# Feed-forward gate and up: wide and narrow products of a weight block in another order

## The reference

```python
def swiglu(h, w_gate, w_up, w_down):
    return (jax.nn.silu(h @ w_gate) * (h @ w_up)) @ w_down

x = x + 0.5 * swiglu(rmsnorm(x, ffn1_norm[i]), ffn1_w_gate[i], ffn1_w_up[i], ffn1_w_down[i])
```

## Time and profile before

| | before |
|---|---|
| median of the three runs | 1577.62 us |
| lowest and highest run | 1577.44, 1578.19 us |
| span of the profiled execution, first to last instruction | 1575.9 us |
| time of the profiled execution itself | not listed apart; the runs lie 1.5 to 2.3 us above its span |
| TensorE busy with products | 1412.2 us, 90% of the span |
| weight loads | 1117.4 us, 71% |
| VectorE, ScalarE, GpSimd | 891.4, 613.8, 33.0 us |
| mean granted TensorE clock | 0.967 of full speed |

### The profile page before, as it was taken

How to read it: one execution, slowest core, us unless ns; L and a number is a source line. 1 busy time by engine, 2 the same in 40 slices (tenths; PEclk the granted TensorE clock), 3 DMA queues, 4 the chain that set the end, 5 groups by cost and what they waited for, 6 DMA issues and landing times.

```text
span 1575.9 us, 25855 instructions
## 1 busy us (share of the span) xinstructions
PE 1412.2 (90%) x10318; PEld 1117.4 (71%) x10318; DVE 891.4 (57%) x1227; ACT 613.8 (39%) x817; POOL 33.0 (2%) x69
## 2 busy tenths in 40 slices
PE   8999999999999999999999999999886666666666
PEld 7888888888888888877788888778653434333333
DVE  5777688577776777765457776777621121121121
ACT  6443465563445543466654344664211001000000
POOL 4000000000000000000010000010000000000000
PEclk9999999999999999999999999999999889989889
DMA  7565543456565555554456556557999999999996
GB/s 239 198 209 191 188 160 134 134 169 218 172 209 164 188 196 197 167 177 142 134 150 214 196 166 211 161 171 271 396 400 427 428 428 428 430 428 429 428 428 291
DMA packets 149044, 396.67 MB, mean 252 GB/s; under 512 B 8003, under 2 KB 106387, under 8 KB 136704
## 3 DMA queue, kind: packets, MB, share of 16 engines
q1 hardware_dynamic: 147424, 392.20, 66.9%
q0 software_dynamic: 1440, 3.72, 1.0%
q10 hardware_dynamic: 128, 0.03, 0.0%
HBM read 393.83 MB, written 1.05 MB: 251 GB/s over the span
## 4 chain that ended last, share of the span: by engine, by line
PE 75%; DMA 19%; DVE 4%; ACT 2%; issue 1%; SPq 0%; ACTq 0%; DVEq 0%; POOL 0%; POOLq 0%
DMA pair_ring<-in_w_exp_up 19%; PE psum L557 17%; PE psum L258 12%; PE psum L260 12%; PE psum L259 12%; PE psum L563 9%; PE psum L2342 6%; PE psum L1024 1%; DVE low L253 1%; PE psum L2369 1%; PE psum L1435 1%; DVE hT L445 1%; ACT hT L435 0%; PE psum L2380 0%; PE psum L424 0%
## 5 line engine op out<-in xcount | busy, mean ns | idle before, releaser
L253 DVE TENSOR_TENSOR low<-raw,high 128x2048 fp32r<-128x2048 f32 x179 | 409.6, 2291 | 193.6 <-ACT high L249 193.1
L249 ACT ACTIVATE high<-raw 128x2048 fp32r<-128x2048 f32 x179 | 341.2, 1910 | 125.1 <-PE psum L563 90.2
L557 PE MATMUL psum<-hT,high 128*128 128x512 f32 x1152 | 288.0, 392 | 0.1
L557 PEld LDWEIGHTS psum<-hT,high 128*128 128x128 f32 x1152 | 209.3, 189 | 39.3 <-DVE low L253 0.4
L2342 PE MATMUL psum<-pair_ring,gain 128*32 128x256 f32 x1984 | 140.2, 445 | 96.1 <-DMA pair_ring<-in_w_exp_up 96.1
L258 PE MATMUL psum<-high,hT 128*128 128x512 f32 x496 | 200.1, 403 | 6.9 <-DVE low L253 4.5
L260 PE MATMUL psum<-high,hT 128*128 128x512 f32 x496 | 194.5, 392 | 0.0
L259 PE MATMUL psum<-low,hT 128*128 128x512 f32 x496 | 193.9, 391 | 0.0
L2342 PEld LDWEIGHTS psum<-pair_ring,gain 128*32 128x32 f32 x1984 | 77.4, 128 | 158.4 <-issue 134.6
L563 PEld LDWEIGHTS psum<-hT,low 128*128 128x128 f32 x1152 | 157.1, 190 | 11.2
L563 PE MATMUL psum<-hT,low 128*128 128x256 f32 x1152 | 160.6, 282 | 0.0
(11 more groups left out here) (356 smaller groups left out, 1452.5 us busy)
## 6 DMA issues: line engine op xcount, KB each, us to landing
pair_ring<-in_w_exp_gate SPq DMA_DIRECT2D x31, 2048.0 KB, 18.9
pair_ring<-in_w_exp_up SPq DMA_DIRECT2D x31, 2048.0 KB, 23.3
pair_ring<-in_w_exp_down SPq DMA_DIRECT2D x31, 2048.0 KB, 24.4
raw<-in_ffn_w_gate SPq DMA_DIRECT2D x88, 512.0 KB, 4.0
raw<-in_ffn_w_up SPq DMA_DIRECT2D x88, 512.0 KB, 5.0
raw<-in_ffn_w_down SPq DMA_DIRECT2D x88, 512.0 KB, 4.3
raw<-in_gla_w_in SPq DMA_DIRECT2D x24, 512.0 KB, 4.5
raw<-in_sb_w_in SPq DMA_DIRECT2D x24, 512.0 KB, 4.7
```

Source lines behind the costliest of these rows:

```text
L249: act.activation(high[:, p % RING, :], raw_of(p), ACT.Copy).then_inc(rounded, 1)
L253: dve.tensor_tensor(low[:, p % RING, :], raw_of(p), high[:, p % RING, :].bitcast(F32), ALU.subtract).then_inc(split, 1)
L557: pe.matmul(to.rearrange("p (o n) -> p o n", o=2), w_high, both_parts, start=kk == 0, stop=False, skip_group_check=True)
```

## The change

The second loop over `k` is taken away. Its body is put into the first one: behind the wide product of (k, i) the narrow product of the same (k, i) is issued. The products, operands, banks, flags and semaphore steps are the same, and the last instruction of a call is still the narrow product of k = 3, i = 1.

```diff
                 kk = 4 * half + k
                 both_parts = hT[:, :, kk * TOKENS:(kk + 1) * TOKENS]
                 for i in range(2):
-                    w_high, _, to = block(k, i)
+                    w_high, w_low, to = block(k, i)
                     pe.matmul(to.rearrange("p (o n) -> p o n", o=2), w_high, both_parts, start=kk == 0, stop=False,
                               skip_group_check=True)
-            for k in range(4):
-                kk = 4 * half + k
-                for i in range(2):
-                    _, w_low, to = block(k, i)
                     ins = pe.matmul(to[:, 0:TOKENS], w_low, hT_high[:, kk, :], start=False, stop=kk == KD - 1,
                                     skip_group_check=True)
             return ins
```

## The result

The changed kernel is slower. Over six runs its median is 1584.48 us, against 1577.53 us for the kernel before: a ratio of 1.0039, 95% interval 1.0028 to 1.0050. In a later group of runs the ratio was 1.0033 (1.0021 to 1.0046). The forecast was 1575.6 us. The measured time lies above the range of 1567.0 to 1582.5 us.

What follows compares the result with a forecast made beforehand. TensorE's own stream was taken to bound the chunks. Pairs of 233.3 + 113.4 = 346.7 ns against 348.4, times 1152, give 2.0 us less: 1577.6 - 2.0 = 1575.6 us, range 1567.0 to 1582.5 us.

Steps and rivals of the forecast that it cites:

- The sum: Calls in the chunks: 346.7 ns a wide-narrow pair against 348.4, times 1152, so 2.0 us less.
- the last stage shifts as a whole: Experts' stage from 1070 us: moves by what the chunks gain or lose, with nothing taken back in it.
- I take 233.3: Calls: a wide product behind a narrow one takes 233.3 ns, bounds 226.7 and 235.8.
- I take 113.4: Calls: a narrow product behind a wide one takes 113.4 ns, bounds 112 and 120.
- cut off by the next narrow: Calls: the disturbance after narrow-to-wide, five products long in the old order, is ended by the following narrow product.
- the bound that I gave (235.8): Calls: upper bound for a wide product behind a narrow one, the old order's second wide distance, 235.8 ns.
- rival 3: Calls: order is indifferent, lateness is paid off in wide products either way; 348.4 ns a pair, 1577.6 us; chance 0.16.
- about 7 ns of a narrow product's 120: Calls: this part goes with loading the next 128-column weight block, for which a narrow product offers little cover.
- a wide product covers its load fully: Calls: a wide product, 227 ns, hides the loading of the next 128-column weight block.
- stays: A chunk's 24 down products: their disturbance behind a narrow product is unchanged, 5.47 us against 5.45.
- Rival 2: Calls: narrow products cover the wide block's load, 233.3 + 120 = 353.3 ns a pair, 5.6 us more, 1583.2; chance 0.18.
- Rival 1: Calls: disturbance only after eight narrow products; 340.1 ns a pair, 9.6 us less, 1567 us; chance 0.33 with nearby cases.

Runs made afterwards that it cites:

- groups of two: Against the kernel before: two wide products, then their two narrow ones, instead of eight and eight in a call; 1577.44 us, ratio 0.9994.
- groups of four: Against the kernel before: four wide products, then their four narrow ones, instead of eight and eight in a call; 1581.47 us, ratio 1.0017.
- of sixteen: Against the kernel before: both hidden blocks' 16 wide products of a piece, then their 16 narrow ones; 1577.13 us, ratio 0.9993.
- the repeated one: The kernel before, unchanged, profiled once more; 1578.86 us, measured once.

## Why the prediction was wrong

**What held.** TensorE's stream alone sets the time of the chunks; no wait appeared in them between 40 and 180 us, and the other engines' work is the same. The sum was right in its form, a difference per pair times 1152, and the last stage shifts as a whole: in the table above the medians follow the chunks within 0.2 us in five rows; in the last they lie 0.5 above and 1.0 below.

**The step that failed** is the price of the pair, put together from two places that the old order has once in a call each: "I take 233.3" and "I take 113.4". The reasons were that the disturbance is "cut off by the next narrow" and that a narrow product behind a wide one finds its weights loaded. The first wide product behind a narrow one in the changed kernel is 232.5, nearly the 233.3 of the old one. But then the disturbance isn't cut off, it goes on: 241 and 236 follow. 241 was above the bound that I gave (235.8); no row of before had it, since there no narrow product ever followed a wide one in a disturbed state. The mean is 236.4 for the wide one, against 233.3. The narrow one is 117.5, 120.0 and 113.3, 116.9 on average, against 113.4. Together 3.1 and 3.5, 6.6 ns a pair too low, which times 1152 is 7.6 us. At 353.3 a pair the change is slower, at 346.7 it would have come out 2 us below before.

The mistake was to treat the distance of a product as a property of its direct neighbour. The rows already spoke against this: after one change five wide products differ from one another, with the same neighbours. What I listed for rival 3, that narrow products with 16-column loads too are unsettled for five places, was the right sign and got too little weight. The reading under the two prices fell too: that about 7 ns of a narrow product's 120 belong to the load of the next block, and that a wide product covers its load fully. With the wide block's load cut to 32 columns the narrow ones stay at 117 to 119, and wide products with 32-column loads alone take 231.7 instead of 226.7.

**The down products.** That their disturbance "stays" was wrong in size: 5.50 us instead of 5.47. They now start from the 241 state and settle after ten products instead of five (241, 238, 233, 236, 224, 231, 236, 228, 233, 231), 36 ns a chunk and 1.3 us in all. Calls: 0.144 us a chunk. Together 0.18 x 36 = 6.5 us; 6.2 in the trace, since the four first chunks, which wait for transposes between the calls, lose less: 91, 146, 13 and 146 ns against 180. The 1.3 us of the down products was a term that the prediction put at nothing.

**The rivals.** Rival 2 had the price to the tenth, 353.3 ns a pair, and the side; with the down products it would have said 1584.5. That was luck in part: its terms were 233.3 and 120 where 236.4 and 116.9 were measured, errors that cancel. And its reason is refuted: it took the 120 ns as the cost of the wide block's load beside the narrow product, and cutting that load to 32 columns left 351.2. Rival 1's 340 was never reached; the nearest is 343.3 with both loads short. Rival 3, that the order is indifferent, fails. The kernel before and groups of two lie close together (16613 and 16587 ns a chunk), but that is a coincidence of two patterns: groups of one take 16793, of four 16687, of sixteen 16573.

**What the runs leave as cause.** With 128-column loads, a stream of one width settles at 120 ns for 256 columns, 173.3 for 384 and 226.7 for 512: each is the columns at 2.4 GHz (106.7, 160, 213.3) plus 13.3 ns. The Trainium skill's "TensorE: Matmul & The Clock Gate", section "Back-to-back issue gap", has plus 2.5 ns at that clock for a single product; the traces don't agree. Alternating 512 with 256 costs 353.3 where the settled parts add up to 346.7, and 512 with 384 costs 406.6 where they add up to 400.0. So alternation of unequal widths costs 6.6 ns a pair over the settled values at both, and alternation of equal widths costs nothing. With settled distances throughout, a chunk would be 32 x 346.7 + 24 x 226.7 = 16533 ns. The changed kernel pays 260 ns over that, 9.4 us in 36 chunks, and the old one already paid 80, 2.9 us, in its four disturbances of 27 ns. The difference is the 6.5 us above.

**What stays open.** Why unequal widths keep the stream unsettled. It isn't the bank, the weight buffer or the access pattern, and the cover of one load doesn't account for it. The loads have a share (343.3 with both short), but short loads also unsettle a stream of equal wide products (231.7). The distances recur with a fixed period for each combination, to the nanosecond and in every call, as two processes would that fall in and out of step; which two, no run here shows. One regularity goes with it: the chunk length of every kernel here, 14 in all, is a whole multiple of 6.67 ns, the time of 16 columns at 2.4 GHz, to within 0.1 ns. The chunk of before (16613.3 ns) has 2492 of them, that of the changed kernel (16793.3) 2519. The settled 120.0, 173.3 and 226.7 are 18, 26 and 34, and three alternating pairs (1060 ns) are 159. Why is not shown.

## What to carry to other kernels

On an engine that is never idle, the order of independent products is worth nanoseconds each, and 1152 times 5 ns, with 36 times 36 ns behind it in the down products, was the whole result. The best order measured here had the longest runs of one shape, joined to the next stage's products of the same shape. It is no steady rule: pairs beat groups of four and of eight, so an order has to be measured. A distance read at the only place where two kinds of instruction meet is not the distance they will have when they meet every time: cost an alternating order from a stretch that alternates, and where the trace has none, keep the range open on both sides.

## What the runs showed of the hardware that I had not expected

- A wide product with a 32-column load, which writes 32 partitions, takes longer (231.7 ns) than one with a 128-column load (226.7), in a stream of nothing else.
- One narrow-to-wide change is felt for five products, and from the worst state for ten.
- Groups of two (348.3 ns a pair) beat groups of four (350.8) and of one (353.3), and their chunk is 27 ns shorter than with the groups of eight of the kernel before.
- The settled distances and all 14 chunk lengths are multiples of 6.67 ns.
- A short stretch at half clock can fall into one execution and not into another of the same kernel, at a cost of 1.2 us (at 12 us in the first profile of the changed kernel), 1.4 us (at 1005 us in that of before) and 1.5 us (at 218 us in the repeated one); it has to be taken out before two spans are compared.
